# Two attention mixers of a three-block transformer: where the last pairs' values go, a fourth probability slot, and the order of the output projection

## Chip, cores and metric

The kernel runs on one core of one Trainium2 chip, as one program and one launch. The metric is device microseconds of that core for the whole program; lower is better.

## What is computed

A sequence of 256 tokens with 1024 features goes through two layers and a closing block. Layer one adds a mixer of eight MLA heads and eight stick-breaking heads, then a SwiGLU; layer two adds a band mixer of sixteen heads, then a SwiGLU; the closing block has 40 heads of attention and gates, which the change doesn't touch. Cut to what matters here:

```python
# first mixer, MLA heads; the stick-breaking heads give o_b
s_a = einsum('bqhd,bkhd->bhqk', q_a[:, t0:kend], k_a[:, :kend]) * scale_a
p_a = softmax(where(chunk_ok, s_a, -inf))
o_a = einsum('bhqk,bkhd->bqhd', p_a, v_a[:, :kend])
h = h + concatenate([o_a, o_b], -1) @ w_out          # 1024 x 1024
# band mixer
p = softmax(scores(q, k) * C_DIM ** -0.5 + bias)     # 16 heads
h = h + (p @ v) @ w_out                              # 1024 x 1024
# between them
h = h + (silu(u @ w_gate) * (u @ w_up)) @ w_down
```

All matrices are float32. Each product with a weight matrix is made of three matmuls: the operands are split into a rounded high part (`w_hi`, `oT_hi`) and a rest (`w_lo`, `oT_lo`), and high*high, high*low and low*high are summed.

## The kernel before

Tokens are two blocks of 128. Weights stream through a ring of three slots in units of 1 MB (128x2048). For each unit SP loads `w_raw` (a load waits until `w_lo` of the slot's last unit is made), ScalarE rounds it to `w_hi` (line 922, `round_unit`), VectorE subtracts to get `w_lo` (line 1538, `split_unit`), and TensorE uses both. ScalarE may write `w_hi` of a unit only when TensorE has counted the unit three before it as used (`unit_used`). In both engines' programs one `slot_step()` does this for the unit two ahead. Every engine works through an order that is written out by hand; there is no planner, and an engine that waits holds back all that stands behind it.

Attention goes by pairs of heads. For a pair `t`: TensorE turns queries and keys (lines 492, 499), ScalarE copies them out (`mla_copy`, line 1121); TensorE makes logits in the two banks of `pair_ps` (`logits`, lines 511, 512); VectorE scales, masks and takes maxima (`maxima`, lines 1622 and 1627), which frees the banks (`logit_read`) and writes the probability slot `logit[:, t % 3]`; ScalarE exponentiates there (`exponentiate`, line 1045, eight instructions); VectorE divides (`normalise`, lines 1668 and 1672, `normed`); TensorE turns the probabilities into `turn_ps` (`turn_probs`, line 524); ScalarE copies one half and VectorE the other to `prT` (`copy_probs`, lines 1051 and 1663); TensorE multiplies by the values (`values`, lines 540 to 542) into `out_ps`, which is the bank `acc[3]`; ScalarE rounds that to `oT_hi` (`round_outputs`, line 1056), VectorE subtracts to `oT_lo` (`outputs`, line 1678), and `out_read` counts that the bank is free.

The output projection sums four units P0 to P3 of two feature tiles each. A piece (`output_piece`, line 612) multiplies one unit with one token block and one or both halves of the 1024 columns; its results stay in `acc[2 * blk + half]` until the last unit. Both halves of a block are 12 matmuls of 512 columns, one half is 6. Half 1 of block 1 is `acc[3]`, the bank of the values: before the change these pieces wait for the values of the last pair, and `unit_used` of P0, P1 and P2 comes only with them. In the first mixer the stick-breaking pairs 0 to 3 give features of P0 and P1, and the MLA pairs (pair 4 to 7 in the counts, called MLA 0 to 3 here) give P2 (0 and 1) and P3 (2 and 3); in the band mixer pairs 0 to 7 give P0 to P3 in turn. After P3 `add_projection` (line 1609) adds to the stream and the SwiGLU begins; its first units are called S0, S1 and S2 here. The ends of the mixers are written out in `first_mixer` and `band_mixer` of each engine, and the steps below are named after their calls.

Of the kernel before, what the change touches and what calls it, by code (L numbers as in the profile page):

```python
# [70 lines left out]
def build_program(nc, x, w_in0, g_cq, w_uq, g_ckv, w_ukv, w_out0, w_qkv, rel_band, w_out1, g_mix, g_ffn,  # L71
# [8 lines left out]
    with ctx:  # L80
# [76 lines left out]
        qkT_ps, out_ps = acc[2], acc[3]  # L157
# [8 lines left out]
        mla_banks = [pair_banks[0], pair_banks[1], side_banks[0], pair_banks[0], pair_banks[1]] + [side_banks[0]] * 3  # L166
# [217 lines left out]
        def _(pe):  # L384
# [130 lines left out]
            def turn_probs(kind, t, pair0):  # L515
                if kind == "mla" or kind == "band":
                    pe.wait_ge(normed, pair0 + (t + 1) - 4)
                else:
                    pe.wait_ge(prob_done, pair0 + (t + 1))
                since(pe, prT_act, pair0 + t)  # L520
                since(pe, prT_dve, pair0 + t)
                for j in range(2):
                    for i in range(3):
                        done = transpose(turn_ps[:, j, P * i:P * i + P], logit[:, t % 3, j, P * i:P * i + P],  # L524
                                         ident[:, :])
                done.then_inc(prT_done, 1)

            def values(kind, t, pair0):
                pe.wait_ge(prT_act, pair0 + (t + 1))
                pe.wait_ge(prT_dve, pair0 + (t + 1))  # L530
                since(pe, out_read, pair0 + t)
                for j in range(2):
# [4 lines left out]
                    if kind != "last":  # L537

                        o = out_ps[HD * j:HD * j + HD, 0:S]
# [4 lines left out]
                    o0, o1 = out_ps[:, HD * j:HD * j + HD], out_ps[:, P + HD * j:P + HD * j + HD]  # L544
# [71 lines left out]
            def band_mixer():  # L616
# [58 lines left out]
            def first_mixer():  # L675
# [51 lines left out]
                def turn_mla(tile, t, i):  # L727
                    before = {3: 1, 4: 2, 5: 3, 6: 6, 7: 7}
# [4 lines left out]
                order = (4, 6, 0, 2)  # L733

# [19 lines left out]
                pe.wait_ge(acc_read, 18)  # L754
                pe.wait_ge(out_read, 2)
                out_piece(0, 0, first=True)
                turn_keys(1)
                logits("mla", 0, 4, 8)
                pe.wait_ge(out_read, 4)
                out_piece(1, 0)  # L760
                turn_keys(2)
                logits("mla", 1, 4, 8)
                turn_keys(3)
                pe.wait_ge(qkT_read, 12)
                out_piece(0, 1, (0,), first=True)
                turn_probs("mla", 0, 4)
                logits("mla", 2, 4, 8)
                out_piece(1, 1, (0,))
                values("mla", 0, 4)
                turn_probs("mla", 1, 4)  # L770
                logits("mla", 3, 4, 8)
                values("mla", 1, 4)
                turn_probs("mla", 2, 4)
                pe.wait_ge(out_read, 6)
                out_piece(2, 0)
                values("mla", 2, 4)
                turn_probs("mla", 3, 4)
# [3 lines left out]
                out_piece(0, 1, (1,), first=True).then_inc(unit_used, 1)  # L781
                out_piece(1, 1, (1,)).then_inc(unit_used, 1)
                out_piece(2, 1).then_inc(unit_used, 1)
# [103 lines left out]
        def _(act):  # L887
# [150 lines left out]
            def exponentiate(kind, t, pair0, head0):  # L1038
                act.wait_ge(max_done, pair0 + (t + 1) - 4)
                pr = logit[:, t % 3, :, :]  # L1040
# [12 lines left out]
            def round_outputs(t, pair0, kt0):  # L1053

                act.wait_ge(out_done, pair0 + (t + 1))
                activation(oT_hi[:, kt0 + t, :], out_ps[:, 0:S], ACT.Copy).then_inc(out_hi, 1)

            def attention_step(kind, s, pair0, head0, kt0=None):
                if kt0 is not None and 3 <= s:
                    round_outputs(s - 3, pair0, kt0)  # L1060
# [63 lines left out]
            def band_mixer():  # L1124
# [12 lines left out]
                def outs(t):  # L1137
                    round_outputs(t, pair0, 0)
# [57 lines left out]
                probs(6)  # L1196
                outs(5)
                probs(7)
                outs(6)
                outs(7)  # L1200
                n.pair = pair0 + 8
                for _ in range(3):
                    slot_step()

            def first_mixer():
# [76 lines left out]
                round_outputs(0, 0, 4)  # L1282
# [5 lines left out]
                round_outputs(1, 0, 4)  # L1288
# [6 lines left out]
                round_outputs(2, 0, 4)  # L1295
# [6 lines left out]
                round_outputs(3, 0, 4)  # L1302
                copy(1)
                for i in range(2, 5):
                    mla_copy(i)
                slot_step()
                for i in range(5, 8):
                    mla_copy(i)
                exponentiate("mla", 0, 4, 0)
                exponentiate("mla", 1, 4, 0)  # L1310
                copy_probs(0, 4)
                exponentiate("mla", 2, 4, 0)
                round_outputs(0, 4, 0)
                copy_probs(1, 4)
                exponentiate("mla", 3, 4, 0)
                round_outputs(1, 4, 0)
                copy_probs(2, 4)
                round_outputs(2, 4, 0)
                copy_probs(3, 4)
                round_outputs(3, 4, 0)  # L1320
                n.pair = 8
                for _ in range(3):
                    slot_step()
# [198 lines left out]
        def _(dve):  # L1522
# [91 lines left out]
            def maxima(kind, t, pair0, head0, bias_of):  # L1614

                pr = logit[:, t % 3, :, :]
                dve.wait_ge(logit_done, pair0 + (t + 1))
                since(dve, prT_done, pair0 + max(t - 2, 0))
# [46 lines left out]
            def normalise(t, pair0):  # L1665
# [3 lines left out]
                for blk in range(TB):  # L1669
                    for j in range(2):  # L1670
                        pr = logit[:, t % 3, j, key_cols(blk)[0]]
# [3 lines left out]
            def outputs(t, pair0, kt0):  # L1675

                dve.wait_ge(out_hi, pair0 + (t + 1))
                v.tensor_tensor(oT_lo[:, kt0 + t, :], out_ps[:, 0:S],
# [20 lines left out]
            def band_mixer():  # L1699
# [9 lines left out]
                def norm(t):  # L1709
                    normalise(t, pair0)  # L1710
# [4 lines left out]
                def outs(t):  # L1715
                    outputs(t, pair0, 0)
# [26 lines left out]
                tops(4)  # L1743
                slot_step()
                tops(5)
                norm(4)
# [10 lines left out]
                probs(6)  # L1757
                outs(5)
                probs(7)
                outs(6)  # L1760
                outs(7)
                n.pair = pair0 + 8
                for _ in range(3):
                    slot_step()
# [53 lines left out]
            def first_mixer():  # L1818
# [49 lines left out]
                outputs(0, 0, 4)  # L1868
                copy_probs(2, 0)
                slot_step(1024)  # L1870
                outputs(1, 0, 4)
# [3 lines left out]
                outputs(2, 0, 4)  # L1875
                slot_step()
                outputs(3, 0, 4)
# [5 lines left out]
                normalise(0, 4)  # L1883
                maxima("mla", 2, 4, 0, mask)
                copy_probs(0, 4)
                normalise(1, 4)
                outputs(0, 4, 0)
                maxima("mla", 3, 4, 0, mask)
                copy_probs(1, 4)
                normalise(2, 4)  # L1890
                outputs(1, 4, 0)
                copy_probs(2, 4)
                normalise(3, 4)
                outputs(2, 4, 0)
                copy_probs(3, 4)
                outputs(3, 4, 0)
                n.pair = 8
                for _ in range(3):
                    slot_step()
# [258 lines left out]
```

## Time and profile before

| what | value |
|---|---|
| median of 3 runs | 1051.57 us (1049.77 to 1051.69) |
| the profiled execution's own time | 1051.47 us |
| its span, first to last instruction | 1049.5 us |
| TensorE matmul busy | 998.5 us, 95% of the span |
| VectorE, ScalarE busy | 60%, 57% |
| mean granted TensorE clock | 0.995 of full speed |
| end of the first mixer's projection | 99.4 to 146.1 us of the span |
| end of the band mixer's projection | about 429 to 460.8 us |

The span is the profile's clock from the first instruction to the last, and all positions below are microseconds in it; the execution's time is 2.0 us longer. A busy share says how long an engine worked, and not that the rest could be saved: for that one looks at each idle stretch and at what ended it.

### The profile page before, as it was taken

Reading aid. Unit: us, or ns where it says so; the run is one execution under the profiler, and the core shown is the slowest. Engines: PE = TensorE matmul, PEld = TensorE weight load, DVE = VectorE, ACT = ScalarE, POOL = GpSimd, SP = SyncE. Lnnn points to the kernel's source line nnn. Section 1 sums busy time; section 2 is a strip of 40 time slices with the busy share of each in tenths; the row PEclk is TensorE's granted clock in tenths of the full one; section 3 lists DMA queues with packets and bytes.
Section 4 is the critical chain, followed back from the end, with each engine's and each line's share of the span. In section 5 each row is a group of like instructions: output and inputs, shape, how many; then the busy total and the mean of one; then the engine's idle time right before and its main releaser. Section 6 shows DMA issues by size and latency. Waiting matters only on the chain.

```text
span 1049.5 us, 13511 instructions
## 1 busy us (share of the span) xinstructions
PE 998.5 (95%) x5026; PEld 816.8 (78%) x5026; DVE 633.9 (60%) x780; ACT 593.0 (57%) x912; POOL 21.3 (2%) x21
## 2 busy tenths in 40 slices
PE   4999789999998999989999998999999998999998
PEld 3888668888887777768888887788787886778876
DVE  3576567555555574665555555668567566766654
ACT  4677464544454564554544454666756575856561
POOL 1000004000000000010000000000000000000000
PEclk9999999999999999999999999999999999999999
DMA  7435156655655433368555655454343333335550
GB/s 232 146 117 200 41 200 193 207 188 173 200 162 198 161 123 121 118 212 291 197 190 171 200 163 197 145 177 161 126 154 120 120 121 121 121 121 200 176 185 40
DMA packets 105691, 170.23 MB, mean 162 GB/s; under 512 B 3843, under 2 KB 65210, under 8 KB 105652
## 3 DMA queue, kind: packets, MB, share of 16 engines
q1 hardware_dynamic: 103040, 161.23, 46.6%
q0 software_dynamic: 2288, 8.37, 2.3%
q8 instruction: 26, 0.43, 0.2%
q10 hardware_dynamic: 324, 0.10, 0.0%
q14 instruction: 13, 0.11, 0.0%
HBM read 168.58 MB, written 1.11 MB: 162 GB/s over the span
## 4 chain that ended last, share of the span: by engine, by line
PE 89%; ACT 5%; DVE 4%; issue 1%; DMA 0%; ACTq 0%; DVEq 0%
PE acc L442 14%; PE acc L402 13%; PE acc L404 12%; PE acc L403 12%; PE pair_ps L404 7%; PE pair_ps L402 7%; PE pair_ps L403 7%; PE acc L612 4%; PE turn_ps L524 2%; PE pair_ps L512 1%; PE acc L492 1%; PE pair_ps L511 1%; ACT w_hi L922 1%; PE turn_ps L460 1%; ACT logit L1045 1%
## 5 line engine op out<-in xcount | busy, mean ns | idle before, releaser
L1538 DVE TENSOR_TENSOR w_lo<-w_raw,w_hi 128x2048 fp32r<-128x2048 f32 (+3 forms) x156 | 351.2, 2256 | 154.6 <-ACT w_hi L922 154.2
L922 ACT ACTIVATE w_hi<-w_raw 128x2048 fp32r<-128x2048 f32 (+3 forms) x156 | 290.3, 1863 | 86.8 <-PE acc L404 47.4
L402 PE MATMUL acc<-w_hi,uT_hi 128*128 128x512 f32 (+3 forms) x552 | 221.3, 401 | 9.9 <-DVE w_lo L1538 6.0
L404 PE MATMUL acc<-w_hi,uT_lo 128*128 128x512 f32 (+3 forms) x552 | 213.8, 387 | 0.0
L403 PE MATMUL acc<-w_lo,uT_hi 128*128 128x512 f32 (+3 forms) x552 | 213.2, 386 | 0.0
L402 PEld LDWEIGHTS acc<-w_hi,uT_hi 128*128 128x128 f32 x552 | 105.2, 191 | 35.1 <-issue 8.9
L402 PE MATMUL pair_ps<-w_hi,uT_hi 128*128 128x512 f32 x320 | 126.6, 396 | 0.0
L404 PE MATMUL pair_ps<-w_hi,uT_lo 128*128 128x512 f32 x320 | 125.0, 391 | 0.0
L403 PE MATMUL pair_ps<-w_lo,uT_hi 128*128 128x512 f32 x320 | 124.7, 390 | 0.0
L404 PEld LDWEIGHTS acc<-w_hi,uT_lo 128*128 128x128 f32 x552 | 104.8, 190 | 21.4
L403 PEld LDWEIGHTS acc<-w_lo,uT_hi 128*128 128x128 f32 x552 | 105.3, 191 | 18.1
L404 PEld LDWEIGHTS pair_ps<-w_hi,uT_lo 128*128 128x128 f32 x320 | 60.1, 188 | 12.8
L1045 ACT ACTIVATE logit<-logit,negmax 128x256 f32<-128x256 f32 (+1 forms) x128 | 56.4, 444 | 24.0 <-DVE negmax L1627 24.0
L403 PEld LDWEIGHTS pair_ps<-w_lo,uT_hi 128*128 128x128 f32 x320 | 60.2, 188 | 12.0
L402 PEld LDWEIGHTS pair_ps<-w_hi,uT_hi 128*128 128x128 f32 x320 | 60.1, 188 | 11.8
L442 PE MATMUL acc<-w_hi,oT_hi 128*128 128x512 f32 x208 | 64.5, 392 | 3.5 <-DVE oT_lo L1922 2.8
L442 PE MATMUL acc<-w_lo,oT_hi 128*128 128x512 f32 x208 | 64.1, 390 | 0.0
L442 PE MATMUL acc<-w_hi,oT_lo 128*128 128x512 f32 x208 | 64.1, 390 | 0.0
L1004 ACT ACTIVATE qkv<-acc,norms 128x512 f32<-128x512 f32 x48 | 32.1, 686 | 56.0 <-PE acc L404 41.7
L1388 ACT ACTIVATE oT_hi<-turn_ps 128x512 fp32r<-128x512 f32 x22 | 13.2, 598 | 78.8 <-PE turn_ps L460 78.8
L1622 DVE SCALAR_TENSOR_TENSOR logit<-pair_ps,bias 128x256 f32<-128x256 f32 (+1 forms) x56 | 28.7, 553 | 46.0 <-PE pair_ps L512 45.1
L1912 DVE SCALAR_TENSOR_TENSOR qkv<-pair_ps,norms,qkv 128x256 f32<-128x256 f32 x40 | 17.5, 480 | 55.7 <-ACT qkv L1384 55.7
(210 smaller groups left out, 1269.0 us busy)
## 6 DMA issues: line engine op xcount, KB each, us to landing
w_raw<-in_w_in SPq DMA_DIRECT2D x46, 1024.0 KB
w_raw<-in_w_gate SPq DMA_DIRECT2D x44, 512.0 KB
w_raw<-in_w_up SPq DMA_DIRECT2D x44, 512.0 KB
w_raw<-in_w_down SPq DMA_DIRECT2D x22, 1024.0 KB
w_raw<-in_w_out SPq DMA_DIRECT2D x12, 1024.0 KB
w_raw<-in_w_qkv SPq DMA_DIRECT2D x16, 512.0 KB
w_raw<-in_w_branch SPq DMA_DIRECT2D x6, 1024.0 KB
w_raw<-in_w_in SPq DMA_DIRECT2D x10, 512.0 KB
```

Source lines behind the costliest of these rows:

```text
L402: mm(o, xh, wh[:, k, :], start=first and k == 0, stop=False)
L403: mm(o, xh, wl[:, k, :], start=False, stop=False)
L404: done = mm(o, xl, wh[:, k, :], start=False, stop=last and k == len(kts) - 1)
L442: done = mm(acc[2 * blk + half][:, :], xp, wp[:, k, 512 * half:512 * half + 512], start=first and k == 0 and i == 0, stop=last and k == 1 ...
L524: done = transpose(turn_ps[:, j, P * i:P * i + P], logit[:, t % 3, j, P * i:P * i + P], ident[:, :])
L612: done = mm(acc[2 * blk + half][:, :], xp, wp[:, k, 512 * half:512 * half + 512], start=first and k == 0 and j == 0, stop=last and k == 1 ...
L922: activation(w_hi[:, slot, 0:width], w_raw[:, slot, 0:width], ACT.Copy).then_inc(hi_done, 1)
L1004: done = activation(dst, src, func, scale=scale)
L1045: done = activation(pr[:, j, cols], pr[:, j, cols], ACT.Exp, bias=negmax8[:, blk, head], accum_out=total8[:, blk, head])
L1538: v.tensor_tensor(w_lo[:, slot, 0:width], w_raw[:, slot, 0:width], w_hi[:, slot, 0:width].bitcast(f32), ALU.subtract).then_inc(lo_done, 1)
L1622: done = v.scalar_tensor_tensor(pr[:, :, cols][:, :, ::-1], pair_ps[:, :, cols][:, :, ::-1], scale, bias_of(t, mask_cols), ALU.mult, ALU.add)
L1912: done = v.scalar_tensor_tensor(hid_g[:, blk, :], gate_ps[:, blk, :], norms[:, norm, 7, blk:blk + 1], hid_e[:, blk, :], ALU.mult, ALU.mult)
```

## The change

Five things are altered; the arithmetic is the same.

- **Bank of the values.** `out_bank` sends the values of all MLA pairs, and of band pairs 4 to 7, to the two banks of `pair_ps` in turn (bank `t % 2`). Before the first of them TensorE waits until VectorE has read the logits of the last pair (`logit_read`). A bank that alternates needs `out_read` of one pair fewer.
- **Fourth slot.** The MLA pairs have four probability slots, three of `logit` and `keeps[0]` in the memory of `bias`, so that maxima wait for no earlier pair's turning.
- **Turning banks.** Keys 1 to 3 of MLA are turned into the banks of `turn_ps` and not of `acc[2]`.
- **Whole blocks.** With `acc[3]` free early, the projection is done in pieces of whole blocks, block 1 of P0 first, and each of P0, P1 and P2 is counted as used when its two blocks are done, between the pairs.
- **Order on ScalarE and VectorE.** The `slot_step()` calls of the last three units stood behind the last outputs; now they stand between the pairs. In the first mixer the exponentials of MLA 0 come before two copies of keys, the copies of probabilities of pair 0 after the exponentials of pair 2, and VectorE's calls are in another order. In the band mixer `norm(4)` moves ahead of a unit and of `tops(5)`.

The core of the diff (calls that only pass the new argument `kind` are cut, and the orders that are written out stand below it in words):

```diff
-        mla_banks = [pair_banks[0], pair_banks[1], side_banks[0], pair_banks[0], pair_banks[1]] + [side_banks[0]] * 3
+        mla_banks = [pair_banks[0], pair_banks[1], side_banks[0], pair_banks[0], pair_banks[1],
+                     turn_banks[0], turn_banks[1], turn_banks[0]]
+        mla_probs = [logit[:, t, :, :] for t in range(3)] + [keeps[0]]
+        def probs_of(kind, t):
+            return mla_probs[t] if kind == "mla" else logit[:, t % 3, :, :]
+        def out_bank(kind, t):
+            return pair_banks[t % 2] if kind == "mla" or (kind == "band" and t > 3) else out_ps
...
# TensorE, values
-                since(pe, out_read, pair0 + t)
+                bank = out_bank(kind, t)
+                since(pe, out_read, pair0 + t if bank is out_ps else pair0 + t - 1)
...
# TensorE, band mixer
-                output_piece(0, 0, 1, (0,), first=True)
-                pe.wait_ge(acc_read, copied + 12)
-                output_piece(0, 0, 0, first=True)
+                output_piece(0, 0, 1, first=True)
+                pe.wait_ge(logit_read, pair0 + 8)
                 vals(4)()
                 probs(6)()
-                output_piece(2, 1, 0)
+                output_piece(0, 0, 0, first=True).then_inc(unit_used, 1)
                 vals(5)()
                 probs(7)()
-                output_piece(2, 1, 1, (0,))
+                output_piece(2, 1, 0)
                 vals(6)()
+                output_piece(2, 1, 1).then_inc(unit_used, 1)
+                vals(7)()
                 pe.wait_ge(out_read, pair0 + 6)
                 output_piece(4, 2, 0)
-                vals(7)()
+                output_piece(4, 2, 1).then_inc(unit_used, 1)
                 n.pair = pair0 + 8
-                output_piece(4, 2, 1, (0,))
                 pe.wait_ge(out_read, n.pair)
-                output_piece(0, 0, 1, (1,), first=True).then_inc(unit_used, 1)
-                output_piece(2, 1, 1, (1,)).then_inc(unit_used, 1)
-                output_piece(4, 2, 1, (1,)).then_inc(unit_used, 1)
```

Written out, the orders after the change (a unit's `slot_step()` makes its `w_hi` on ScalarE and its `w_lo` on VectorE; P(i, b) is the piece of unit Pi and block b):

```
TensorE, first mixer, after the turns of queries 0 to 3 and keys 0:
  P(0,1); keys 1; logits 0; P(0,0), P0 used; keys 2; logits 1; P(1,0) half 0; keys 3; logits 2; P(1,0) half 1;
  turn_probs 0; logits 3; P(1,1), P1 used; wait for logit_read of pair 3; values 0; turn_probs 1; values 1;
  turn_probs 2; wait for outputs 0 and 1; P(2,0); values 2; turn_probs 3; P(2,1), P2 used; values 3;
  wait for outputs 2 and 3; P(3,0); P(3,1)
ScalarE, first mixer, after the copy of ukv 1, block 0:
  copy queries 0, 1; outputs of stick-breaking pair 3; copy queries 2; ukv 1, block 1; copy queries 3, keys 0;
  unit P2; copy keys 1; exp 0; copy keys 2, 3; exp 1; exp 2; probs 0; unit P3; exp 3; outputs 0; probs 1;
  outputs 1; probs 2; unit S0; outputs 2; probs 3; outputs 3; unit S1
VectorE, first mixer:
  unit P2; maxima 0, 1; norm 0; maxima 2; norm 1; probs 0; maxima 3; probs 1; norm 2; outputs 0; unit P3;
  probs 2; outputs 1; norm 3; unit S0; probs 3; outputs 2, 3; unit S1
VectorE, band mixer, from pair 4 on (ScalarE's three units stand in the same places):
  unit; maxima 4; norm 4; unit P0; maxima 5; norm 5; probs 4; unit P1; maxima 6, 7; probs 5; norm 6; unit P2; norm 7;
  outputs 4; probs 6; unit P3; outputs 5; probs 7; outputs 6; unit S0; outputs 7; unit S1
```

## Rows read from the trace of the kernel before

**Rows 1.** The page's first part: TensorE's busy time, share, instructions.

```profile
PE 998.5 (95%) x5026; PEld 816.8 (78%) x5026; DVE 633.9 (60%) x780; ACT 593.0 (57%) x912; POOL 21.3 (2%) x21
```

**Rows 2.** Stretches: length, busy PE, PEld, DVE, ACT, POOL, granted clock, DMA, GB/s.

```profile
99.60:146.10 46.50, 38.57 (x215) 30.82 (x214) 26.42 (x51) 21.04 (x51) 0.00 (x0) 0.96 0.25 77
...
120.90:123.50 2.60, 0.00 (x0) 0.00 (x1) 2.56 (x6) 0.50 (x3) 0.00 (x0) 0.95 0.00 0
123.50:127.00 3.50, 3.47 (x20) 3.13 (x21) 1.51 (x7) 1.81 (x8) 0.00 (x0) 0.55 0.02 5
...
418.90:421.40 2.50, 0.19 (x2) 0.00 (x0) 2.38 (x8) 1.14 (x5) 0.00 (x0) 1.00 0.74 216
```

**Rows 3.** Timeline of TensorE, first mixer's end; idle time before in brackets.

```profile
99.36 0.71 PE L612 MATMUL acc<-w_hi,oT_hi 128*128 128x512 f32 x2
...
123.53 0.66 PE L540 MATMUL acc<-prT,heads 128*64 128x128 f32 x2 [2.67 <-issue]
...
140.32 0.73 PE L612 MATMUL acc<-w_hi,oT_hi 128*128 128x512 f32 x2 [0.31 <-DVE w_lo L1538]
```

**Rows 4.** Chain that ended last, first mixer's end: start, length, what.

```profile
106.85 0.44 PE acc L499 x4
107.29 0.22 PE pair_ps L511 x2
...
108.60 0.45 PE acc L499 x4
109.08 0.59 ACT bias L1121
...
118.70 0.84 PE turn_ps L524 x6
...
125.53 1.37 PE turn_ps L524 x6
126.90 2.75 PE acc L612 x12
129.65 0.36 PE acc L540 x2
...
130.76 0.39 ACT oT_hi L1056
131.18 0.42 DVE oT_lo L1678
131.60 0.53 DVE prT L1663
...
136.02 1.93 ACT w_hi L922
137.97 2.30 DVE w_lo L1538
...
140.32 5.75 PE acc L612 x24
146.09 1.30 DVE h L1609 x2
```

**Rows 5.** The same chain in the band mixer's end.

```profile
412.26 1.85 ACT logit L1045 x8
...
419.21 1.01 DVE negmax L1627 x2
420.34 1.02 DVE logit L1672 x4
```

**Rows 6.** Timelines of TensorE and VectorE, band mixer's end.

```profile
421.41 0.88 PE L524 MATMUL turn_ps<-ident,logit 128*128 128x128 f32 x6 [2.32 <-DVE logit L1672]
...
428.79 0.50 PE L511 MATMUL pair_ps<-qkT 64*128 64x128 f32 x4
...
455.04 0.73 PE L612 MATMUL acc<-w_hi,oT_hi 128*128 128x512 f32 x2 [1.68 <-DVE w_lo L1538]
...
426.17 1.01 DVE L1622 SCALAR_TENSOR_TENSOR logit<-pair_ps,bias 128x256 f32<-128x256 f32 x2
```

More of the change, by code:

```diff
@@ L733, in first_mixer, with turn_probs_and_values @@
                 order = (4, 6, 0, 2)
+                def turn_probs_and_values(t):
+                    if t == 0:
+                        pe.wait_ge(logit_read, 8)
+                    values("mla", t, 4)
+                    turn_probs("mla", t + 1, 4)
                 def out_piece(i, blk, halves=(0, 1), first=False, last=False):
@@ L753, in first_mixer @@
                 turn_keys(0)
-                pe.wait_ge(acc_read, 18)
-                pe.wait_ge(out_read, 2)
-                out_piece(0, 0, first=True)
+                pe.wait_ge(lo_done, n.unit + 1)
+                pe.wait_ge(out_read, 4)
+                pe.wait_ge(qkT_read, 4 + 3)
+                out_piece(0, 1, first=True)
                 turn_keys(1)
                 logits("mla", 0, 4, 8)
-                pe.wait_ge(out_read, 4)
-                out_piece(1, 0)
+                pe.wait_ge(acc_read, 18)
+                out_piece(0, 0, first=True).then_inc(unit_used, 1)
                 turn_keys(2)
                 logits("mla", 1, 4, 8)
+                out_piece(1, 0, (0,))
                 turn_keys(3)
+                logits("mla", 2, 4, 8)
+                out_piece(1, 0, (1,))
                 pe.wait_ge(qkT_read, 12)
-                out_piece(0, 1, (0,), first=True)
                 turn_probs("mla", 0, 4)
[L767 to L770, printed above, removed]
                 logits("mla", 3, 4, 8)
-                values("mla", 1, 4)
-                turn_probs("mla", 2, 4)
+                out_piece(1, 1).then_inc(unit_used, 1)
+                turn_probs_and_values(0)
+                turn_probs_and_values(1)
                 pe.wait_ge(out_read, 6)
                 out_piece(2, 0)
-                values("mla", 2, 4)
-                turn_probs("mla", 3, 4)
+                turn_probs_and_values(2)
+                out_piece(2, 1).then_inc(unit_used, 1)
                 values("mla", 3, 4)
@@ L1137, in outs @@
                 def outs(t):
-                    round_outputs(t, pair0, 0)
+                    round_outputs("band", t, pair0, 0)
                 slot_step()
@@ L1199, in band_mixer @@
                 outs(6)
+                slot_step()
                 outs(7)
                 n.pair = pair0 + 8
-                for _ in range(3):
-                    slot_step()
+                slot_step()
             def first_mixer():
@@ L1709, in norm @@
                 def norm(t):
-                    normalise(t, pair0)
+                    normalise("band", t, pair0)
                 def probs(t):
@@ L1715, in outs @@
                 def outs(t):
-                    outputs(t, pair0, 0)
+                    outputs("band", t, pair0, 0)
                 for _ in range(4):
@@ L1743, in band_mixer @@
                 tops(4)
+                norm(4)
                 slot_step()
                 tops(5)
-                norm(4)
                 norm(5)
@@ L1760, in band_mixer @@
                 outs(6)
+                slot_step()
                 outs(7)
                 n.pair = pair0 + 8
-                for _ in range(3):
-                    slot_step()
+                slot_step()
                 add_projection()
@@ L1882, in first_mixer @@
                 maxima("mla", 1, 4, 0, mask)
-                normalise(0, 4)
+                normalise("mla", 0, 4)
                 maxima("mla", 2, 4, 0, mask)
+                normalise("mla", 1, 4)
                 copy_probs(0, 4)
-                normalise(1, 4)
-                outputs(0, 4, 0)
                 maxima("mla", 3, 4, 0, mask)
                 copy_probs(1, 4)
-                normalise(2, 4)
-                outputs(1, 4, 0)
+                normalise("mla", 2, 4)
+                outputs("mla", 0, 4, 0)
+                slot_step()
                 copy_probs(2, 4)
-                normalise(3, 4)
-                outputs(2, 4, 0)
+                outputs("mla", 1, 4, 0)
+                normalise("mla", 3, 4)
+                slot_step()
                 copy_probs(3, 4)
-                outputs(3, 4, 0)
+                outputs("mla", 2, 4, 0)
+                outputs("mla", 3, 4, 0)
                 n.pair = 8
-                for _ in range(3):
-                    slot_step()
+                slot_step()
                 n.qk = 1
```

78 lines of the change are left out of this document (40 added, 38 removed).

## Prediction, on record before the changed kernel ran

> **What bounds the kernel now.** I read the page first: TensorE works 95% of the span [rows 1], so a change of order can win only TensorE's idle time and the time it works at a low clock. Then the waits of TensorE showed which idle stretches lie at the two ends that the change touches, and the windows gave their sum. In the first mixer's end, from 99.6 to 146.1, TensorE is busy 38.57 of 46.5 us: 7.9 us idle [rows 2]. The largest piece is 2.67 us before the values of MLA 1 [rows 3]. It also costs clock: in the last part of that gap the granted clock falls (0.95), in the next 3.5 us it is 0.55 [rows 2], that is nearly all at 1.2 GHz, and the values and turning that start at 123.53 end at 126.90, 3.37 us, where values take 129.65 to 130.76, 1.1, and a turning 0.84 [rows 4]. So the low level costs 3.37 - 1.95 = 1.4 us. In the band mixer's end the idle stretches are 2.32 us before the turning of pair 4's probabilities, ended by a division on VectorE, and 1.68 us before P3, ended by its `w_lo` [rows 6]. In all 7.9 + 1.4 + 4.0 = 13.3 us could be had at most; the SwiGLU behind each end starts after the residual addition of block 1 (146.09, 1.30 us) [rows 4], whose wait stays.
>
> **The first mixer, worked out.** TensorE's instructions are the same in number; only places and waits differ. Durations from end to end: a whole block 2.75, half a block half of it, 1.38; the turning of one key tile 0.44; logits 107.29 to 108.60, 1.31; probabilities turned 0.84; values 1.1 [rows 4]. On the others: `w_hi` 1.93, `w_lo` 2.30, outputs 0.39 and 0.42, copy of probabilities 0.53 (I take it for ScalarE's too) [rows 4]; exponentials 1.85, maxima 1.01 and 1.01, a division 1.02 [rows 5, 6] and some 0.2 for its reciprocal.
>
> The turns of queries and keys 0 end near 99.6, where P(0,0) began before [rows 3]; now P(0,1) does. It needs the copy of queries 2 first; the copy is now ahead of a block of `ukv`, takes 0.59 like the one in [rows 4] and is ready at about 99.3, so nothing is late. Then TensorE's ends run: P(0,1) 102.4, keys 102.8, logits 104.1, P(0,0) 106.9, keys 107.3, logits 108.6, half block 110.0, keys 110.4, logits 111.7, half block 113.1, turning of MLA 0 114.0, logits 115.3, P(1,1) 118.0, values 119.1, turning of MLA 1 119.9. No wait ends late in there. VectorE begins maxima 0 at 105.1 (unit P2 is 0.4 later), maxima 1 at 108.6 when its logits exist, divides MLA 0 until 111.9, makes maxima 2 to 113.9, divides MLA 1 to 115.1, copies, and ends maxima 3 at 117.6, where the banks have been free since 116.6, ahead of the 118.0 at which values 0 want one. ScalarE exponentiates MLA 0, 1, 2 at 107.1, 111.0 and 114.0 and copies half of MLA 0 at 116.3. The fourth slot and the banks of `turn_ps` therefore cost nothing and let this stretch run without those parts of the 7.9 us that lay ahead of the 2.67.
>
> Now the moved units come in. ScalarE makes `w_hi` of P3 from 116.3 to 118.2, and exponentials 3 behind it end at 120.0; outputs 0 follow, then its half of MLA 1's copy to 120.9. Values 1 wait for that: **0.9 us idle**, 120.9 to 122.0, turning of MLA 2 until 122.8. VectorE meanwhile copies to 120.5, divides to 121.7, outputs 0 to 122.1, and then `w_lo` of P3, whose source has been ready since 118.2, to 124.4. Behind it in VectorE's queue stand copy 2 and outputs 1, and P(2,0) is what waits for outputs 1: 124.4 + 0.5 + 0.4 = 125.2. **2.4 us idle.** After it P(2,0) ends 128.0, values 129.1, turning 129.9, P(2,1) 132.7, values 3 133.8; here S0's unit is in front of nothing TensorE waits for (`w_lo` to 128.3, its wait at 129.9). Then outputs 3, 0.39 + 0.42 and the hand-overs, **0.9 us idle**, as before the change; P3's weights are long there. 134.7 + 5.75 [rows 4] = 140.4, against 140.32 + 5.75 = 146.07: **5.7 us**. As a check, idle time falls from 7.9 to 4.2 and the low clock's 1.4 is gone, 5.1; the other 0.6 is that TensorE restarts four times less, and a restart costs 0.1 to 0.2.
>
> Unit S1's `w_lo` ends about 138 and the residual addition starts on time. Loads of SP start when `w_lo` frees a raw slot: S2's comes some 16 us earlier, in a stretch where the DMA engines stand at 0.00 and 0.02 [rows 2], so it meets nothing. GpSimd's load of band bias starts 6 us sooner, and nobody waits for it.
>
> **The band mixer, worked out.** `norm(4)` needs exponentials 4, over at 412.26 + 1.85 = 414.1 [rows 5], and VectorE has nothing until P0's `w_hi` at 416.0, so it runs there free, and the turning of pair 4 no longer waits: 2.3 us. But logits 7 stand behind maxima 6, which start at 426.17 and release the banks at 427.2 [rows 6], and nothing in the chain to 426.17 (units P0 and P1, maxima 5, exponentials 5) gets earlier. TensorE would be there at 428.79 - 2.4 = 426.4 and waits 0.8: of the 2.3 us some **1.5** are left. P0 is used at 436.4, after three whole steps (P(0,1), values 4 with a turning, P(0,0)) behind the turning of pair 5; P3's `w_hi` and `w_lo` are ready at 440.7, long before P3 begins at 451. The unit S0 stands in front of outputs 7 on both engines: ScalarE from 445.1 (P1 used) to 447.0, VectorE to 449.4, outputs 7 at 449.8, while TensorE works on P(2,0) and P(2,1) to 451.6. That cover is 1.8 us thick. So the whole **1.7** before P3 goes too, and its restart 0.1: **3.3 us**.
>
> **Not shown by the trace.** Values into a bank of `pair_ps` and copies out of it: the nearest rows are logits into `pair_ps` and the same copies from `acc`, and matmul time there goes by columns and not by bank, so 0; if each pair's copies took 0.1 more, 8 pairs would hide all but the last, 0.2. A probability slot in the memory of `bias`: 0, bound 0.1 by the same reasoning. How VectorE's three instructions behind P3's `w_lo` really fall: if the hand order slips and the `w_lo` comes before outputs 0 can start, nothing changes for TensorE by more than 0.5; were the 2.4 us not there, 8.1 instead of 5.7.
>
> Sum: 5.7 + 3.3 = **9.0 us**. The profiled execution took 1051.47; the forecast is 1042.5. The median of the three runs is 0.1 higher, which I leave out. A measurement tells about 0.2%, 2.1 us, from no change.
>
> **Rivals.**
> 1. *The clock falls again in the new gap* (0.30). The pair 0.9 and 2.4 us between 119.9 and 125.2 with 1.9 us of work between is near to the case with the fall, 2.67 us [rows 3] with a shorter gap of the 7.9 us close ahead, while 2.32 us after steady work had no fall, clock 1.00 [rows 2]. It would cost what it cost there, 1.4 to 1.7 us: 1043.9 to 1044.2. The lowest of the runs before, 1.8 us under the median, may be one without the fall. The Trainium skill (TensorE: Matmul & The Clock Gate, section Part 1) says that the low clock is the resting state and only activity releases it; by that rule such a pair of gaps puts it at risk, and the time would be this rival's 1043.9 and not 1042.5. The trace shows both outcomes.
> 2. *The queues hold more than I see* (0.10): moved units delay exponentials 3 or outputs 1 by one more `w_hi` or `w_lo`, 1.9 to 2.3 us in one mixer or in both: 1045 to 1047. For it: both queues are now full between 116 and 125. Against: the units' sources are ready each time.
> 3. *The order only moves the idle time* (0.04): the SwiGLU or the weight stream takes back what the ends win, 1050 to 1052. Against: in the 12 steps behind each end TensorE shows no wait for weights.
> 4. *Slower* (0.04): TensorE enters the last four blocks at 1.2 GHz and stays there, because gaps of 0.9 us follow. Each us of work at that level costs one more; the 9.0 us are used up when 9 us of work run low, and if all from 125.2 to 140.4 did, 14 us, it would be 1042.5 + 14 = 1056. Against: before the change the level was low for 3.5 us only.
> 5. *More than forecast* (0.07): the gap before P(2,0) or the one before logits 7 is smaller, 1040 to 1041.
>
> The forecast itself has 0.45, its own range 1041.3 to 1043.5. From 1040.6, a little into rival 5, to 1045.4, past rival 1 and the near part of rival 2, lie about 8 in 10. Faster than 1049.4: 0.92; within 0.2%: 0.04; slower: 0.04.
>
> **What would show it.** In the profile of the changed kernel: TensorE without idle time from 99.6 to about 119.9; then about 0.9 us ended by ScalarE's copy of probabilities, 2.4 us before a projection piece ended by `oT_lo` with a `w_lo` ahead of it on VectorE, 0.9 us before P3; clock 1.00 or about 0.5 behind the second gap. The first mixer's last piece ends near 140.4. In the band mixer no wait before pair 4's turning, 0.8 us before logits 7 on VectorE's first instruction of maxima, none before P3. The prediction is wrong if outputs 7 are late there, if ScalarE waits for `unit_used` in front of exponentials or outputs, or if the SwiGLU steps get idle time that they didn't have.

## The result, and the profile after the change

The changed kernel takes 1046.64 us (median of 20 runs, 1042.77 to 1052.56), the kernel before, on the same chip, 1053.43 (20 runs, 1049.56 to 1057.60). The ratio is 0.995, with a 95% interval of 0.993 to 0.9971: 5.3 us faster, where 9.0 was forecast. The two medians lie 6.8 us apart, more than the ratio's 5.3; below, a gain against the kernel before is worked out from the ratio where medians aren't named. As an absolute time the forecast was 1042.5, with a range of 1041.3 to 1043.5, and 1046.64 is above it. The profiled execution took 1046.46 us, with a span of 1044.5 and a mean granted clock of 0.990 (before: 1051.47, 1049.5, 0.995). TensorE's work is what it was, as the page's first line shows against [rows 1]:

```profile
PE 998.5 (96%) x5026; PEld 817.6 (78%) x5026; DVE 633.4 (61%) x780; ACT 592.0 (57%) x912; POOL 21.6 (2%) x21
```

TensorE's timeline of the changed kernel, all rows with a wait that the change moved or made (the bracket is the idle time before the row, and what ended it):

```profile
120.54 0.40 PE L550 MATMUL pair_ps<-prT,heads 128*64 128x128 f32 x2 [0.70 <-ACT prT L1062]
...
124.95 0.73 PE L622 MATMUL acc<-w_hi,oT_hi 128*128 128x512 f32 x2 [2.45 <-DVE oT_lo L1693]
...
136.18 0.73 PE L622 MATMUL acc<-w_hi,oT_hi 128*128 128x512 f32 x2 [0.93 <-DVE oT_lo L1693]
...
423.24 0.50 PE L520 MATMUL pair_ps<-qkT 64*128 64x128 f32 x4 [1.02 <-DVE logit L1637]
```

These answer to [rows 3, 6]. The reader is to see that the four waits are those of the forecast: 0.70 for 0.9, 2.45 for 2.4, 0.93 for 0.9, 1.02 for 0.8, each ended by the engine that was named, and that the two of 2.32 and 1.68 us in the band mixer are gone. What VectorE does ahead of the second one is as written too:

```profile
121.48 0.42 DVE L1693 TENSOR_TENSOR oT_lo<-pair_ps,oT_hi 128x256 fp32r<-128x256 f32 x1
121.82 2.28 DVE L1553 TENSOR_TENSOR w_lo<-w_raw,w_hi 128x2048 fp32r<-128x2048 f32 x1
124.02 0.55 DVE L1678 COPY prT<-turn_ps 128x384 f32<-128x384 f32 x1
124.48 0.42 DVE L1693 TENSOR_TENSOR oT_lo<-pair_ps,oT_hi 128x256 fp32r<-128x256 f32 x1
```

The windows of the changed kernel (columns as in [rows 2]) show what the waits did to the clock, in the first mixer and in two stretches of the closing block:

```profile
99.60:146.10 46.50, 40.58 (x231) 32.85 (x231) 28.59 (x56) 24.14 (x60) 1.18 (x1) 0.96 0.35 117
123.00:127.00 4.00, 2.05 (x8) 1.65 (x9) 3.96 (x9) 1.83 (x2) 0.00 (x0) 0.91 0.42 126
127.00:130.00 3.00, 3.00 (x13) 2.08 (x13) 1.23 (x1) 0.00 (x0) 0.00 (x0) 0.55 0.70 221
...
660.00:664.00 4.00, 2.96 (x9) 2.37 (x10) 4.00 (x3) 3.97 (x5) 0.00 (x0) 0.77 0.51 156
...
872.00:878.00 6.00, 2.69 (x9) 2.31 (x10) 4.74 (x7) 3.36 (x6) 0.00 (x0) 0.65 0.00 1
```

Behind the 2.45 us the granted clock is 0.55 again, nearly all at 1.2 GHz, as it was behind the 2.67 us before [rows 2]. In the closing block, whose instructions the change leaves alone, it falls behind a wait of 2.19 us at 661.04 that was 0.59 us before, and at one of 3.53 us at 875.31. The kernel before has falls in that block too, but elsewhere or shorter: 0.66 over 655 to 660, ahead of the short wait, and 0.57 over 881 to 885.

Where the 5.0 us of the two profiled executions lie follows from the starts of the parts (before, after):

| point | before | after | won so far |
|---|---|---|---|
| first SwiGLU starts | 149.86 | 145.73 | 4.1 |
| band mixer starts | 340.45 | 336.40 | 4.1 |
| second SwiGLU starts | 464.58 | 457.03 | 7.6 |
| closing block starts | 655.25 | 647.72 | 7.5 |
| late in it | 1022.17 | 1017.19 | 5.0 |

The first mixer gave 4.1 for the forecast's 5.7, the band mixer 3.5 for 3.3, and the closing block took back 2.5.

### The profile page after: what moved, and what is told of

The parts are those of the page before. It is cut to its first block, busy times and chain, and to the rows that moved or that the text cites. A ratio compares the mean times of both kernels' runs of the same rounds, so it can differ in the third digit from the quotient of the medians.

```text
span 1044.5 us, 13512 instructions
## 1 busy us (share of the span) xinstructions
PE 998.5 (96%) x5026; PEld 817.6 (78%) x5026; DVE 633.4 (61%) x780; ACT 592.0 (57%) x912; POOL 21.6 (2%) x21
## 4 chain that ended last, share of the span: by engine, by line
PE 88%; ACT 5%; DVE 4%; issue 1%; DMA 0%; ACTq 0%; DVEq 0%
PE acc L451 14%; PE acc L411 12%; PE acc L413 12%; PE acc L412 12%; PE pair_ps L413 7%; PE pair_ps L411 7%; PE pair_ps L412 7%; PE acc L622 4%; PE turn_ps L533 2%; PE pair_ps L521 1%; PE acc L501 1%; ACT w_hi L933 1%; PE pair_ps L520 1%; PE turn_ps L469 1%; ACT uT_hi L964 1%
## 5 line engine op out<-in xcount | busy, mean ns | idle before, releaser
L1056 ACT ACTIVATE logit<-logit,negmax 128x128 f32<-128x128 f32 (+1 forms) x124 | 54.7, 444 | 23.3 <-DVE negmax L1642 23.3
```

The source lines that it names most:

```text
L1056: done = activation(pr[:, j, cols], pr[:, j, cols], ACT.Exp, bias=negmax8[:, blk, head], accum_out=total8[:, blk, head])
```

## The experiments

All are compared with the kernel before on the same chip. Four questions were asked in turn: is it the two ends, the clock, something that differs between executions, and what is still to be had. "Fill" stands for transposes of the identity matrix, which nobody reads, put in front of a wait of TensorE so that it works there. They are extra work, not computation left out.

**The changed kernel again (e1_again).** No edit.

> The changed kernel once more, beside the kernel before on the same chip. Theory A (the clock decides the rest: the waits at the two ends are what the prediction worked out, and what is missing against 9.0 us is time at 1.2 GHz, some of it in the closing block, whose place differs from execution to execution): the idle times at the ends stay within 0.1 us of 0.7, 2.45, 0.93 and 1.02, the low stretches lie elsewhere or have other lengths than in the first profile, and the time is 4 to 8 us below the kernel before. Theory B (something in the changed kernel costs time in every execution): a low stretch or a new wait at the same place as in the first profile, with the same length, and the difference again near 5 us.

Measured: 1047.22 (12 runs, 1042.94 to 1051.66), ratio 0.9951 (0.9931 to 0.997). In its profile (1047.04 us) the wait of 2.46 us is there and the clock behind it is whole:

```profile
124.60:128.00 3.40, 3.35 (x17) 2.56 (x19) 3.29 (x6) 0.00 (x0) 0.00 (x0) 1.00 0.85 268
```

From the first weight matmul to the first SwiGLU it takes 125.11 us, and 130.84 in the kernel before: 5.73, the forecast's 5.7. So the sum was right for an execution without the fall after and with it before. But this execution isn't faster than the other: it lost its clock at 334.5, 662, 864 and 877. The time fits theory A (4 to 8 us) and theory B (near 5 us) alike; the fall at 126 that didn't come again speaks for A, and those at 662 and 877 are near the places of the first profile.

**Each end alone (e2_first_only, e3_band_only).** The one has the new first mixer and the old band mixer, the other the reverse.

> The first mixer as after the change, the band mixer as before it. By the terms of the prediction 5.7 us without a fall of the clock behind the 2.4 us gap, 4.1 us with it. Theory A: the SwiGLU behind the first mixer starts 4.1 or 5.7 us earlier than before, and the total is 2 to 6 us lower. Theory B: the total is lower by under 2 us, with the loss after the mixer at one place.

> The band mixer as after the change, the first mixer as before it. The prediction gave 3.3 us, the first profile shows 3.5 us between the starts of the two SwiGLUs. Both theories: 3.4 us there. Theory A: the total 2 to 4 us lower. Theory B, if the band mixer is what costs later: under 1 us lower.

Measured: 1049.94 (ratio 0.9985, 0.9971 to 0.9998) and 1048.63 (0.998, 0.9962 to 0.9997), so 1.6 and 2.1 us, together less than the 5.3 of both. (By medians it is 1.9 and 3.2.) For e2 that is under what theory A gave; in its profile the stretch from the first weight matmul to the first SwiGLU is 126.43 us, 4.4 under the old one, and there are falls at 126, 460 and 877. The band stage is 120.63 us long in e3 as in the changed kernel, 3.50 under the 124.13 before. The first mixer of e3 is the one of before, and there the clock is 1.00 behind the same 2.67 us:

```profile
120.90:124.50 3.60, 1.91 (x18) 1.54 (x18) 2.93 (x10) 2.13 (x9) 0.00 (x0) 1.00 0.02 5
124.50:128.50 4.00, 3.85 (x24) 3.03 (x24) 1.74 (x7) 0.49 (x1) 0.00 (x0) 1.00 0.00 0
```

From the first weight matmul to the first SwiGLU it takes 129.14 and not 130.84. The 1.4 us of low clock in [rows 2] is a thing that some executions of the kernel before have and others don't. Over the profiles of this study the 2.67 us wait had a fall behind it in two of three, and the 2.45 us wait in three of five.

**The gap made smaller, or filled (e4_lo_later, e5_fill_gap).** In e4 VectorE makes P3's `w_lo` behind the outputs that P(2,0) waits for:

```diff
                 outputs("mla", 0, 4, 0)
-                slot_step()
                 copy_probs(2, 4)
                 outputs("mla", 1, 4, 0)
                 normalise("mla", 3, 4)
                 slot_step()
+                slot_step()
```

> The changed kernel with VectorE's unit P3 in the first mixer behind copy 2, outputs 1 and division 3. If that w_lo is what makes TensorE's 2.45 us wait before the first piece of P2: the wait is 1.0 us and not 2.45. If the gap of 2.45 us is what lowers the clock there (rival 1): the clock stays at 1.00 behind it, and the first mixer ends 1.4 + 1.6 = 3.0 us earlier than in the first profile of the changed kernel. If the clock falls whatever the gap: only 1.4 us earlier. In the total 1.4 to 3 us below the changed kernel.

e5 fills the gap instead:

```diff
+                pe.wait_ge(out_read, 5)
+                fill(pair_banks[0], 18)
```

> The changed kernel with 18 extra transposes of the identity on TensorE, into a bank of pair_ps that is free then, inside the 2.45 us wait before the first piece of P2. The wait for outputs 1 stays, so the gap is only filled (0.11 us each, 2.0 us). If the clock behind the gap falls because TensorE stands idle: clock 1.00 behind it in the profile, the wait left is about 0.4 us, the first mixer ends 1.6 us earlier than where the clock fell, and the median is 1 to 2 us below the changed kernel. If the clock falls for another reason: 0.5 behind it as before, no gain.

Measured, in 6 runs each: e4 1041.37 (ratio 0.9915, 0.9891 to 0.9939), e5 1042.66 (0.9909, 0.9878 to 0.9941). TensorE's timeline and window, of e4 and then of e5:

```profile
123.79 0.72 PE L622 MATMUL acc<-w_hi,oT_hi 128*128 128x512 f32 x2 [0.98 <-DVE oT_lo L1693]
...
123.80:127.00 3.20, 3.20 (x14) 2.41 (x15) 3.17 (x7) 1.35 (x1) 0.00 (x0) 1.00 0.00 0
```

```profile
123.95 0.73 PE L626 MATMUL acc<-w_hi,oT_hi 128*128 128x512 f32 x2 [0.49 <-DVE oT_lo L1699]
...
123.95:127.00 3.05, 3.05 (x13) 2.28 (x14) 3.02 (x6) 0.00 (x0) 0.00 (x0) 1.00 0.91 263
```

e4 takes 1.5 us out of the wait, as the queue says, and in both the clock stays up. Both won more than was expected. The fill alone doesn't bring outputs 1 sooner and still takes 4.0 us off the changed kernel's median (1046.64), more than the 1.3 to 1.7 that one fall costs; so either the fall wasn't all, or it brings something else with it.

**All long waits filled (e6_fill_all_after, e7_fill_all_before).** The same, and also 16 transposes ahead of the wait at 661 and 26 ahead of the one at 875; in the kernel before, 20 ahead of the values of MLA 1.

> The changed kernel with that filling and two more in the closing block: 16 transposes before the second chunk (wait of 2.2 us for ScalarE's copy of qkv) and 26 before the turning of the last group (wait of 3.5 us). Theory A (what is missing against the forecast is time at 1.2 GHz behind waits): the waits shrink to under 1 us, no low clock behind these three places, the spread of the times narrows, and the median falls to 1041 to 1042, that is 4 us or more below the changed kernel's. Theory B (a cost that has nothing to do with the clock): within 1 us of e5.

> The kernel before with the same three fillings (20 transposes in its 2.67 us wait before values 1). Theory A: its median falls too, to 1048 to 1049.5, and the difference between this one and e6 is what the traces give for the two ends without falls: 4.3 us for the first mixer and 3.5 us for the band mixer, 7.8 us in all. Theory B: the difference stays near 5 us.

Measured: e6 1041.30 (6 runs; 0.9886, 0.9858 to 0.9914), e7 1051.18 (12 runs; 0.9985, 0.9968 to 1.0002). With the falls at these places taken from both, the medians are 9.9 us apart: the gain of the two ends is there, and larger than I expected; I had put e7 too low. e7's profiled execution took 1055.79, and its rows of ScalarE, VectorE, GpSimd and TensorE and one window show a cause that the theory lacked:

```profile
154.98 1.92 ACT L933 ACTIVATE w_hi<-w_raw 128x2048 fp32r<-128x2048 f32 x1 [1.69 <-PE turn_ps L408]
...
153.33 2.29 DVE L1549 TENSOR_TENSOR w_lo<-w_raw,w_hi 128x2048 fp32r<-128x2048 f32 x1 [1.98 <-ACT w_hi L933]
156.93 10.70 DVE L1549 TENSOR_TENSOR w_lo<-w_raw,w_hi 128x2048 fp32r<-128x2048 f32 x1 [1.32 <-ACT w_hi L933]
...
156.43 9.04 POOL L369 TENSOR_TENSOR bias<-bias,m_chunk 128x4096 f32<-128x4096 f32 x1 [9.84 <-DMA bias<-in_rel_band]
...
169.20 1.12 PE L464 MATMUL turn_ps<-ident,qkv 128*128 128x128 f32 x4 [3.44 <-DVE qkv L1928]
...
147.40:151.40 4.00, 3.80 (x10) 3.00 (x11) 3.37 (x14) 2.89 (x9) 0.00 (x0) 0.58 1.03 371
```

GpSimd adds the mask to the band bias in one instruction of 9.04 us. It began 0.5 us ahead of a `w_lo`, and that took 10.70 us, where 2.3 is usual. This is called a collision below. TensorE then waited 3.44 us for a product of VectorE (`qkv`) that stands behind this `w_lo` in its order. The Trainium skill (SBUF — State Buffer, section Who interferes with whom) says that a VectorE instruction with two inputs in SBUF contends with a GpSimd instruction that reads SBUF, that the pair of ports they share is an exclusive lock, and that the order of issue decides who blocks. The trace agrees: the addition ends at 165.47, and the `w_lo` at 167.63, 2.2 us later, as if it had begun only then.

What put GpSimd first in e7 stands in the same rows. The granted clock is 0.58 at the start of the SwiGLU, so TensorE used up its weights later, ScalarE's `w_hi` waited 1.69 us for it, and the second `w_lo` began 3.60 us behind the first. In the kernel before they begin 2.21 apart; at that distance this one would have begun at 155.54, 0.89 us ahead of the addition. In the changed kernel's own profile VectorE was first, by 0.2 us:

```profile
151.46 4.49 DVE L1553 TENSOR_TENSOR w_lo<-w_raw,w_hi 128x2048 fp32r<-128x2048 f32 x2 [1.98 <-ACT w_hi L933]
160.95 6.07 DVE L1553 TENSOR_TENSOR w_lo<-w_raw,w_hi 128x2048 fp32r<-128x2048 f32 x1 [0.20 <-ACT w_hi L933]
...
153.89 10.98 POOL L378 TENSOR_TENSOR bias<-bias,m_chunk 128x4096 f32<-128x4096 f32 x1 [9.16 <-DMA bias<-in_rel_band]
```

The second of the two `w_lo` begins 2.21 us into the first row, at 153.67, and the addition at 153.89. By the same reckoning VectorE's lead was 0.55 us in the kernel before, 1.37 in e3, and 0.22, 0.28 and 0.30 in the changed kernel, e1 and e2, that is in the executions with the new first mixer. The other profiles with it spread further, from 0.02 in e6 to 0.90 in e15. Of 32 executions of the changed kernel 14 took 1048.49 us or more, and the others at most 1047.24; of 109 of the kernel before, 8 took over 1055. None of the profiles of the changed kernel itself is of the upper group.

**The collision forced (e13_early_add).** Changed kernel, with GpSimd's load of band bias issued one block earlier:

```diff
-            pool.wait_ge(h_ready, 2)
+            pool.wait_ge(h_ready, 1)
```

> The changed kernel with the load of the band's bias issued after the residual addition of block 0 and not of block 1, some 2.2 us earlier. In the profiles of the changed kernel GpSimd's addition was ready 0.2 to 0.3 us after VectorE had begun its second w_lo of the SwiGLU, in those of the kernel before 0.5 to 1.4 us after. Theory C (the slow executions are those in which it is ready before that w_lo starts): now it is so in nearly all executions, a w_lo of 9 to 11 us stands in the profile, TensorE waits 3 us or more behind it, and the median goes up to 1049 to 1052, where the slow executions of the changed kernel were. Against it: median and spread as in e1, the w_lo late but not waited for.

Measured: 1049.18 (12 runs, 1047.50 to 1050.55), ratio 0.9967 (0.9953 to 0.9982).

```profile
149.77 13.34 DVE L1553 TENSOR_TENSOR w_lo<-w_raw,w_hi 128x2048 fp32r<-128x2048 f32 x2 [1.98 <-ACT w_hi L933]
...
150.22 10.74 POOL L378 TENSOR_TENSOR bias<-bias,m_chunk 128x4096 f32<-128x4096 f32 x1 [9.47 <-DMA bias<-in_rel_band]
...
164.68 1.11 PE L469 MATMUL turn_ps<-ident,qkv 128*128 128x128 f32 x4 [4.06 <-DVE qkv L1934]
```

The two `w_lo` take 13.34 us for 4.49, TensorE waits 4.06, and the first SwiGLU lasts 196.1 us instead of 190.6: the collision costs 5.5, with the fall of the clock behind that wait. All twelve times lie in or near the upper group of the changed kernel, and the median is what theory C gave.

**The collision made harmless (e9_split_after, e10_split_before).** GpSimd's addition in eight pieces, in the changed kernel and in the one before:

```diff
-            pool.tensor_tensor(band, band, m_chunk[:, :].unsqueeze(1).broadcast_to([P, 16, S]),
-                               ALU.add).then_inc(band_ready, 1)
+            for part in range(8):
+                some = band[:, 2 * part:2 * part + 2, :]
+                pool.tensor_tensor(some, some, m_chunk[:, :].unsqueeze(1).broadcast_to([P, 2, S]),
+                                   ALU.add).then_inc(band_ready, 1)
...
-                dve.wait_ge(band_ready, 1)
+                dve.wait_ge(band_ready, 8)
```

> The changed kernel with GpSimd's addition of the chunk mask to the band's bias (one instruction of 9 us at the start of the first SwiGLU, read and written in SBUF) in eight pieces. In the profile of e7 this addition began just before a w_lo of VectorE, the w_lo took 10.7 us and not 2.3, and TensorE waited 3.4 us more; in the other profiles it fell later and a w_lo took 6.1 us without a wait of TensorE. Theory C (the slow executions of both kernels, 1051 to 1052.5 of the changed one, 1053.6 to 1057.5 of the one before, are those in which the addition falls before a w_lo that is needed soon): no w_lo over 4.6 us, the slowest runs of the changed kernel gone, median 1 to 2 us lower than its 1046.6 to 1047.2. Theory A (they come from the clock alone): times and spread as in e1.

> The kernel before with the same eight pieces. Theory C: runs over 1055 gone, median 0 to 1.5 us lower. Theory A: as the kernel before.

Measured: e9 1043.88 (9 runs, 1043.16 to 1046.76), ratio 0.9924 (0.9899 to 0.9949); e10 1051.85 (12 runs, 1049.66 to 1054.66), 0.999 (0.997 to 1.0011). VectorE and GpSimd in e9:

```profile
153.81 2.32 DVE L1555 TENSOR_TENSOR w_lo<-w_raw,w_hi 128x2048 fp32r<-128x2048 f32 x1 [1.35 <-ACT w_hi L935]
...
165.56 3.43 DVE L1555 TENSOR_TENSOR w_lo<-w_raw,w_hi 128x2048 fp32r<-128x2048 f32 x1 [0.53 <-ACT w_hi L935]
...
152.69 14.15 POOL L380 TENSOR_TENSOR bias<-bias,m_chunk 128x512 f32<-128x512 f32 x8 [9.25 <-DMA bias<-in_rel_band]
```

Here too the clock was down at the SwiGLU's start (0.50 over 145 to 147) and the second `w_lo` 1.35 us late, so that GpSimd was first, at 152.69. That would have been a collision, but no `w_lo` is longer than 3.43 us, and none of the 9 times is in the upper group. That is 8.0 us below the kernel before, with the 2.45 us wait and its fall still there (0.59 in the profile). Before the change the pieces win nothing that can be told, but its few times above 1055 are gone too. With the pieces in both kernels the change is worth 8.0 us by medians and 6.9 by the ratios.

**Pieces and fills (e11_split_fill_after, e12_split_fill_before).** Both edits in both kernels.

> e6 (all three waits filled in the changed kernel) with the eight pieces. Both causes out of the way: median 1040 to 1041.5, spread under 3 us.

> e7 (waits filled in the kernel before) with the eight pieces. If the fillings and the pieces take out what differs from execution to execution: median 1048.5 to 1049.5, spread under 4 us and not 7, and the difference to e11 is the 7.8 us that the traces give for the two ends. If something else is left: spread as in e7.

Measured: 1041.23 (6 runs; 0.9891, 0.9855 to 0.9926) and 1051.12 (12 runs; 0.9982, 0.9959 to 1.0005). The difference, 9.9 us again (9.6 by the ratios), is what was measured for the change with neither the collision nor the falls at the filled places. It is more than the 7.8 that I expected, and e12 is above the times I gave. The two profiled executions don't show the surplus: they lie 7.7 us apart, with 4.0 in the first mixer and 3.4 in the band mixer, and each has one fall at a SwiGLU's start (144 in e11, 463 in e12). Where the other 2 us of the medians come from wasn't settled.

**A better order (e8_tight, e14_tight_split, e15_tight_split_fill).** e8 keeps the change and moves what the traces showed to be early: units P3 and S0 stand on ScalarE and VectorE behind everything that P(2,0) needs, VectorE's division 2 stands ahead of copy 1 and outputs 1 ahead of copy 2, P(2,1) has the values of MLA 3 between its halves, and VectorE's maxima 6 stand ahead of unit P1. Its core:

```diff
-                out_piece(2, 1).then_inc(unit_used, 1)
+                out_piece(2, 1, (0,))
                 ...
+                out_piece(2, 1, (1,)).then_inc(unit_used, 1)
```

e14 adds the eight pieces of e9, e15 also the two fills of the closing block.

> The changed kernel with an order that follows from the waits of its trace: first mixer, ScalarE's units P3 and S0 behind copy 2, VectorE's division 2 ahead of copy 1 and unit P3 behind copy 2, outputs 1 and division 3, TensorE's block 1 of P2 split around values 3; band mixer, maxima 6 ahead of unit P1. The waits of 0.7, 2.45, 0.93 and 1.02 us all shrink to under 0.4 us. Without falls of the clock at the ends 4 to 5 us less than the changed kernel's same ends, and with its fall gone 6: the median near 1040, 1 to 2 us below e4. If units S0 and S1 are then late, a new wait for w_lo at the start of the SwiGLU.

> e8 (the tighter order) with the addition in eight pieces. No collision: slowest run under 1042, median 1037.5 to 1038.5. The idle stretch that e8's profile shows before values 3 (1.0 us) stays.

> e14 with the two fillings of the closing block. If a fall of the clock behind the waits of 2.2 and 3.5 us costs what the profiles show (1.6 to 2.6 us together where it comes): median 1036 to 1037, 1 to 2 us below e14.

Measured, in 6, 4 and 5 runs: e8 1038.15 (0.987, 0.9841 to 0.9898), e14 1037.79 (0.9858, 0.9826 to 0.9891), e15 1037.06 (0.9858, 0.9829 to 0.9886). In e8 the waits of 2.45, 0.93 and 1.02 are gone; left, against what I expected, are the 0.70 and one of 1.01 before the values of MLA 3. From the first weight matmul to the first SwiGLU it takes 122.35 us; the changed kernel takes 126.41 with the fall and 125.11 without it (e1). The band mixer takes 119.57 for 120.63. So the order itself gives some 3.8 us, and the rest is falls and collisions that didn't come. These beat both kernels, by about 14 and 9 us. Between the three nothing can be told.

## Why the prediction was wrong

**Right: the order of the work.** All four waits came at their places, with lengths within 0.22 us of the forecast and the releaser named, and the stages had the forecast sizes where the clock was as assumed: 5.73 us for 5.7 (e1), 3.50 for 3.3. Nothing waited for banks or for the fourth slot, the band's outputs 7 were in time, and the SwiGLU behind each end kept its length, except in executions with the collision.

**The step that failed first: "GpSimd's load of band bias starts 6 us sooner, and nobody waits for it."** Nobody waits for it by a semaphore, but its addition holds a `w_lo` that is issued after it, and the prediction gave this no term at all. Its own last sign of being wrong, idle time in the SwiGLU steps that they didn't have, is what e7 and e13 show (3.44 and 4.06 us). What a collision costs is shown: 5.5 us when forced (e13). How often it comes is argued from the times: 14 of 32 executions of the changed kernel are in that group, and none of 9 with the pieces. An estimate from these counts is (14/32 - 8/109) x 5.5 = 2.0 us of the missing 3.7; the limit of 1055 for the kernel before is my choice.

Why it comes more often with the new first mixer is open. The addition had been 0.55 us behind the second `w_lo` of the SwiGLU, and is 0.2 to 0.3 behind in three executions with that mixer; GpSimd waited 9.16 us for the load instead of 9.50, and SP's loads, which ran beside it before, are over sooner (the one at 140.29 starts at 124.13). But leads of 0.02 to 0.90 all ended without a collision, and the two unforced profiles in which GpSimd was first, e7 and e9, both have the low clock at the SwiGLU's start, which put the `w_lo` back by 1.4 us. That is more than most leads, of either kernel. So there the fall decided, and not a few tenths.

**The second: "the low clock's 1.4 is gone".** Rival 1 came true in the profile, 0.55 behind the 2.45 us. From the first weight matmul on that first mixer takes 126.41 us, 4.4 under the old, and e1's without the fall 125.11: the fall cost 1.3, near the rival's 1.4 to 1.7, and is most of what lies between 4.1 and 5.7. I had booked the baseline's fall as a sure gain because its one profile had it. e3 shows the old mixer without it, and then the old stage takes 129.14, so without falls on both sides the first mixer wins 129.14 - 125.11 = 4.0. With falls about as frequent before (two of three) as after (three of five), some 1.4 us of the 9.0 should not have been in the sum. With the collision's 2.0 that is 3.4 of 3.7. Both are estimates from few executions, and by the medians only 2.2 us are missing. The two ends without falls, 4.0 and 3.5, add up to 7.5, between the 6.9 and 8.0 that e9 and e10 give.

Rival 1 also took the 2.32 us wait of the band mixer as a case without a fall. Its window in [rows 2] ends where the wait ends and can't show that, and in e10 the clock is 0.57 over 422 to 426, behind the same wait.

**Not in the forecast: the closing block.** It took 2.5 us back in the profiled execution by falls behind its own waits. In e2, e3, e4 and e9 it takes 367.0 to 368.0 us as before (366.92), in the changed kernel 369.47 and in e1 370.31. Whether the change makes these falls likelier is open; where the waits are filled it takes 365.4 to 365.5 in both kernels, and 365.5 too in e8, which has no fill and no fall there. That all the falls are chance between executions is argued from the same wait having both outcomes.

Rival 2 (queues), 4 (low clock to the end) and 5 (more than forecast) did not occur: no wait was more than 0.22 us longer than forecast, and the clock was down for some 3 us. Rival 3 (idle only moved) came true in part: a collision makes TensorE idle in the SwiGLU, by 3.44 us in e7.

## What to carry to other kernels

When a long GpSimd instruction starts within a microsecond or two of VectorE's two-input ones, look at the starts in several executions, and at what a fall of the clock would do to them (1.4 us here), or cut it into pieces: with eight pieces the gain was 8.0 us where it had been 5.3. A fall of the clock in one profile is a chance and not a term: look for the same wait in a second execution before its cost is booked. Put the weight work of later units behind all that TensorE waits for next; that reordering and its smaller companions took another 6 us off the medians, with the pieces in both (e9, e14), some 3.8 of which its trace shows at the two ends.

## What the hardware did that I had not expected

- One wait of the same length, at the same place, has a fall behind it in one execution and none in the next (2.67 us: clock 0.55 before, 1.00 in e3; 2.45 us: 0.55 after, 1.00 in e1).
- GpSimd's addition of 128x4096 makes a `w_lo` of 2.3 us into one of 10.70 (e7) or some 11 (e13, 13.34 for two); the same work in eight pieces takes GpSimd 14.15 us instead of 10.98 and leaves none longer than 3.43 (e9).
- A low clock at the SwiGLU's start (0.58 over 147.4 to 151.4), where the longest wait ahead was 1.34 us, moved a `w_lo` by 1.4 us and so changed which of two engines issued first (e7). The first SwiGLU took 197.1 us there, 192.2 in e9 with such a fall and the pieces, and 190.6 with neither.
- The times of the changed kernel fall in two groups, up to 1047.24 and from 1048.49 us; with the pieces (e9) the upper one is gone.
